# Two of eight contraction pairs of w_up by seven block products, in blocks of 1024 features

## The chip, the cores and the metric

The kernel runs on one core of one Trainium2 chip. The time is the device time of that core in microseconds (us). Three runs of the kernel before gave 1325.3, 1325.52 and 1325.8 us; the median is 1325.52 us.

## The reference

One layer of a hybrid decoder block on x of 256 tokens by 2048 features, all in float32. It computes an RMSNorm, a wide input projection, two token mixers (an mLSTM of 4 heads and a block-sparse attention of 8 heads), a gated merge, `x = x + merged @ w_out`, and then the MLP, which is the part at stake here:

```
hn = rms_norm(x, norm_mlp)                                # (256, 2048)
x  = x + square(relu(hn @ w_up)) @ w_down                 # w_up (2048, 8192), w_down (8192, 2048)
```

The two MLP products are 256x2048x8192 each; together they are the larger half of all the arithmetic.

## The kernel before

**Precision.** Every float32 operand of a product is split into a high part (what the matrix engine's reduced float32 format keeps) and a low part (the rest). A product is then three matmuls: high by high, high by low, low by high. The weights come from HBM into `raw` (4 slots of 1 MB), ScalarE copies the high part into `w_hi`, VectorE subtracts it from the raw value into `w_lo`. Both are rings of `RING = 4` slots, and one slot holds 128 x 1024 numbers.

**Steps.** The work of TensorE (PE) is a row of steps with one running number g. For each step ScalarE (ACT) makes w_hi (L477, L716), VectorE (DVE) makes w_lo (L785, L1117), and PE uses both. ACT waits for `w_used`, so that it writes step g only when PE has finished step g-4. DVE waits for `hi_made` of step g, and PE for `lo_made` of step g. All three engines run their own program strictly in order. Everything else that ACT and DVE must do (norms, reading PSUM, squares, transposes, splitting features) is a job that is written out by hand at a given step, ahead of that step's copy or subtraction: the functions `jobs`, `up_jobs`, `first_sums`, `add_shared`, `add_own`.

**The MLP.** It is done in two halves f = 0, 1 of 4096 features each. In a half, w_up comes first, in 8 blocks of 512 features (j). A block has 8 steps; a step is two contraction tiles of 128 by 512 columns and takes 12 matmuls (two row tiles of tokens, two contraction tiles, three products, `half_rows`, L1244 to L1246). The results of a block stand in two PSUM banks, and blocks alternate between banks 4, 5 and 6, 7. Then ACT takes the relu with the norm's scale from PSUM (L730), squares it in 16 pieces of 32 partitions, which also moves blocks between partitions (L740), DVE transposes within 32 x 32 blocks into banks 0 to 3 (L1148), ACT copies the high part (L746) and DVE subtracts for the low part (L1153).

**Seven products.** w_down is done in two passes (n = 0, 1) of 1024 output columns over all eight banks. The contraction is in 16 pairs of tiles. Ten pairs are whole: 2 steps of 12 matmuls. Six pairs (`SEVEN`) use seven block products in place of eight, after Strassen and Winograd: the 2 x 2 blocks are (two token tiles) x (two contraction tiles) for the features and (two contraction tiles) x (two column halves) for the weights. Such a pair has 4 steps of 6, 3, 6 and 6 matmuls, 21 in place of 24. Its price is on DVE: three sums of the weights (`first_sums`, L1136 and L1138, and L1121), 3.5 in place of 2 subtractions of 1024 columns, sums of features (L1157 to L1161 and L1166, L1167), and the adding up of shared banks (`add_shared`). Four of the banks (`OWN`) hold results of their own, the four of `SHARED` hold terms that several results share.

## Time and profile before

| | |
|---|---|
| median of three runs | 1325.52 us |
| the profiled execution | 1325.57 us |
| its span, first to last instruction | 1323.8 us |
| PE busy | 1319.8 us (100% of the span), 5962 matmuls |
| DVE busy | 1003.3 us (76%) |
| ACT busy | 792.2 us (60%) |
| granted TensorE clock | 1.00 throughout |
| DMA | 259.57 MB, 196 GB/s mean |

How to read it: matmuls are pipelined, so each lasts some 0.39 us while one starts every 0.23 us; an engine that is 100% busy by the count need not be at its peak. "Idle before" is the time that an engine sat idle ahead of an instruction, and the arrow names what ended it. A time of a group's row is the mean of one instruction; in a timeline the first number is the start, the second the duration of the row, and xN says how many instructions were merged into it.

### The profile page before, as it was taken

The page shows a single profiled execution, that of the slowest core. Times are in us where ns is not written, and L with a number is a line of the kernel's source. Part 1 is how long each engine was busy: PE and PEld are TensorE (multiplying, and loading weights), DVE is VectorE, ACT ScalarE, POOL GpSimd, SP SyncE. Part 2 cuts the span into 40 slices and gives each one's busy share as a digit, 9 for nine tenths or more (in the row PEclk, how much of TensorE's full clock was granted, in tenths as well). Part 3 has the DMA queues.
Part 4 walks back from the last instruction along what each step waited for, and adds up shares of the span by engine and source line. Part 5 has one row for each costly group of instructions (what it writes and reads, how often), then busy time and mean ns, then how long its engine had stood idle before and what let it go on. Part 6 is the DMA issues. An engine that isn't in the chain of part 4 may idle for free.

```text
span 1323.8 us, 15784 instructions
## 1 busy us (share of the span) xinstructions
PE 1319.8 (100%) x5962; PEld 1096.2 (83%) x5962; DVE 1003.3 (76%) x1314; ACT 792.2 (60%) x1129; POOL 16.5 (1%) x31
## 2 busy tenths in 40 slices
PE   9999999999999999999999999999999999999999
PEld 8988888888888888888888888888888888888887
DVE  6788699777477874999856565999865565689986
ACT  6656554566545444354587878555536878775553
POOL 0101000000000000000000000000000000000000
PEclk9999999999999999999999999999999999999999
DMA  9656555555556665564665665565666666546563
GB/s 318 203 181 212 193 192 183 191 174 176 179 170 197 242 212 194 173 212 170 219 195 191 191 192 189 183 212 184 218 222 191 191 193 192 196 165 208 196 216 129
DMA packets 115173, 259.57 MB, mean 196 GB/s; under 512 B 4334, under 2 KB 7452, under 8 KB 114844
## 3 DMA queue, kind: packets, MB, share of 16 engines
q1 hardware_dynamic: 115068, 258.57, 59.4%
q8 instruction: 47, 0.77, 0.2%
q14 instruction: 26, 0.21, 0.0%
q10 hardware_dynamic: 32, 0.01, 0.0%
HBM read 256.46 MB, written 2.10 MB: 195 GB/s over the span
## 4 chain that ended last, share of the span: by engine, by line
PE 100%; DVE 0%; issue 0%
PE ps L1244 23%; PE ps L1246 23%; PE ps L1245 23%; PE ps L1254 8%; PE ps L1255 8%; PE ps L1256 8%; PE ps L1399 1%; PE ps L1380 1%; PE ps L1348 1%; PE ps L1344 1%; PE ps L1346 1%; PE ps L1354 0%; PE ps L1419 0%; PE ps L1470 0%; PE ps L1436 0%; PE ps L1418 0%
## 5 line engine op out<-in xcount | busy, mean ns | idle before, releaser
L785 DVE TENSOR_TENSOR w_lo<-raw,w_hi 128x1024 fp32r<-128x1024 f32 (+1 forms) x349 | 424.5, 1224 | 246.3 <-ACT w_hi L477 241.7
L477 ACT ACTIVATE w_hi<-raw 128x1024 fp32r<-128x1024 f32 (+1 forms) x349 | 368.2, 1062 | 319.9 <-PE ps L1246 302.5
L1244 PE MATMUL ps<-w_hi,xT 128*128 128x512 f32 x1088 | 425.7, 391 | 0.0
L1246 PE MATMUL ps<-w_hi,xT 128*128 128x512 f32 x1088 | 423.5, 389 | 0.0
L1245 PE MATMUL ps<-w_lo,xT 128*128 128x512 f32 x1088 | 423.3, 389 | 0.0
L1246 PEld LDWEIGHTS ps<-w_hi,xT 128*128 128x128 f32 x1088 | 204.2, 188 | 42.8
L1244 PEld LDWEIGHTS ps<-w_hi,xT 128*128 128x128 f32 x1088 | 204.3, 188 | 41.9
L1245 PEld LDWEIGHTS ps<-w_lo,xT 128*128 128x128 f32 x1088 | 204.3, 188 | 41.8
L716 ACT ACTIVATE w_hi<-raw 128x1024 fp32r<-128x1024 f32 (+1 forms) x152 | 147.9, 991 | 85.9 <-PE ps L1256 69.8
L1117 DVE TENSOR_TENSOR w_lo<-raw,w_hi 128x1024 fp32r<-128x1024 f32 (+1 forms) x152 | 168.0, 1138 | 41.3 <-ACT w_hi L716 39.4
L740 ACT ACTIVATE gate<-gate 32x256 f32<-32x256 f32 x256 | 106.0, 414 | 3.4
L1256 PE MATMUL ps<-w_hi,merged 128*128 128x512 f32 (+1 forms) x210 | 81.5, 388 | 0.0
L1255 PE MATMUL ps<-w_lo,merged 128*128 128x512 f32 (+1 forms) x210 | 81.5, 388 | 0.0
L1254 PE MATMUL ps<-w_hi,merged 128*128 128x512 f32 (+1 forms) x210 | 81.3, 387 | 0.0
L1255 PE MATMUL ps<-w_lo,branch 128*128 128x512 f32 x208 | 81.1, 390 | 0.0
L1256 PE MATMUL ps<-w_hi,branch 128*128 128x512 f32 x208 | 81.1, 390 | 0.0
L1254 PE MATMUL ps<-w_hi,branch 128*128 128x512 f32 x208 | 81.0, 389 | 0.0
L803 DVE STREAM_TRANSPOSE ps<-attn 32x256 f32<-32x256 f32 (+1 forms) x176 | 71.7, 407 | 2.9
L716 ACT ACTIVATE w_hi<-gate 128x1024 fp32r<-128x1024 f32 x24 | 25.5, 1062 | 45.0 <-PE ps L1256 45.0
L1244 PE MATMUL ps<-w_hi,branch 128*128 128x512 f32 x128 | 49.8, 389 | 0.0
L1245 PE MATMUL ps<-w_lo,branch 128*128 128x512 f32 x128 | 49.8, 389 | 0.0
L1246 PE MATMUL ps<-w_hi,branch 128*128 128x512 f32 x128 | 49.8, 389 | 0.0
(243 smaller groups left out, 1396.2 us busy)
## 6 DMA issues: line engine op xcount, KB each, us to landing
raw<-in_w_in_dram SPq DMA_DIRECT2D x73, 1024.0 KB, 5.1
raw<-in_w_up_dram SPq DMA_DIRECT2D x64, 1024.0 KB, 5.3
raw<-in_w_down_dram SPq DMA_DIRECT2D x64, 1024.0 KB, 5.1
raw<-in_w_out_dram SPq DMA_DIRECT2D x16, 1024.0 KB, 5.1
raw<-in_w_branch_b_dram SPq DMA_DIRECT2D x8, 1024.0 KB, 5.3
raw<-in_w_branch_a_dram SPq DMA_DIRECT2D x8, 1024.0 KB, 5.3
raw<-in_w_in_dram SPq DMA_DIRECT2D x4, 1040.0 KB, 9.0
rows<-in_x_dram SPq DMA_DIRECT2D x1, 2048.0 KB, 10.0
```

What stands on the lines that cost most here:

```text
L477: act.activation(dst[:, k % RING, :, :], src[:, k // 2, KH * (k % 2):KH * (k % 2) + KH, :], ACT.Copy).then_inc(hi_made, 1)
L716: act.activation(dst[:, 0:src.shape[-1]], src, ACT.Copy).then_inc(hi_made, 1)
L740: last = act.activation(moved[32 * q:32 * q + 32, r // 32, :, :, :], read[r:r + 32, q, :, :, :], ACT.Square)
L785: dve.tensor_tensor(lo[:, k % RING, :, :], src[:, k // 2, KH * (k % 2):KH * (k % 2) + KH, :], hi[:, k % RING, :, :].bitcast(F32), ALU.subt ...
L803: turned = dve.transpose(dst[q:q + 32, :, :, r:r + 32], src[r:r + 32, :, :, q:q + 32])
L1117: dve.tensor_tensor(lo, src, hi.bitcast(F32), ALU.subtract).then_inc(lo_made, 1)
L1244: pe.matmul(o, hi, w_hi[:, s, i, :], start=first, stop=False)
L1245: pe.matmul(o, hi, w_lo[:, s, i, :], start=False, stop=False)
L1246: last = pe.matmul(o, lo, w_hi[:, s, i, :], start=False, stop=end)
L1254: pe.matmul(ps[:, bank, out], a_hi, w_hi[:, s, c, cols], start=start, stop=False)
L1255: pe.matmul(ps[:, bank, out], a_hi, w_lo[:, s, c, cols], start=False, stop=False)
L1256: return pe.matmul(ps[:, bank, out], a_lo, w_hi[:, s, c, cols], start=False, stop=end)
```

## The change

A half f now has six blocks q. Blocks 0 to 3 are w_up in 1024 features each (before: eight of 512), and blocks 4 and 5 are the two passes of w_down. A w_up block goes over all eight banks, like a pass of w_down: eight pairs of contraction tiles, of which pairs 3 and 5 (`X_SEVEN`) go by seven products in 4 steps, and the other six are whole, in 2 steps each. So a w_up block has 20 steps (s0 to s19 in what follows). In block 0 the order of pairs is 0, 1, 2, 4, 3, 5, 6, 7, so steps s8 to s15 are the two seven-product pairs; in blocks 1 to 3 it is 0 to 7 and they are s6 to s9 and s12 to s15. Block 5 has its pairs in a new order with the same pattern of whole and seven.

What comes with it:

- `x_jobs`: the sums of the features hn of pairs 3 and 5, once for each half (x = 0, 1), at steps s5 and s6 of the first block 0 and at s18 and s20 of block 5 of the first half. DVE adds high and low part (128x512), makes four sums of 128 columns, ACT copies the high parts (128x512), DVE subtracts the low parts (128x512).
- the jobs on the results of block b: at its step s19 ACT copies a shared bank (`up_first`) and DVE makes four additions of 512 columns; at s3 of the next block DVE adds the own banks (2 of 128x1024); at s4 ACT takes the relu (2 of 128x1024, from SBUF); from s5 on ACT squares in 16 pieces of 32x512, two in a step of a whole pair and one in a step of a seven-product pair, so until s16 (in block 4 until s15); in the two steps after the last square DVE transposes (128x1024 each, within SBUF; before into PSUM); ACT's high parts one step after each; DVE's low part and the sums for w_down 3 and 5 steps after the last square, and the low parts of those sums 5 and 7 steps after it.
- ACT and DVE run one loop over all steps of the MLP; SP's loads of w_up are written out (they were a loop) and bring two tiles of 1024 columns in place of four tiles of 512, again 1 MB each.

```diff
 SEVEN = (3, 5, 7, 9, 11, 13)
-ORDER = ((0, 1, 2, 4, 6, 3, 5, 8, 7, 10, 9, 11, 12, 13, 14, 15), (0, 3, 1, 5, 2, 7, 4, 9, 6, 11, 8, 13, 10, 12, 14, 15))
-PARTS = [[4 if i in SEVEN else 2 for i in ORDER[n]] for n in range(2)]
-DOWN = sum(PARTS[0]) + sum(PARTS[1])
-FB = 8 + DOWN // 8
-OWN, SHARED = (4, 0), (0, 4)
+X_SEVEN = (3, 5)
+UP = 4
+ORDER = ((0, 1, 2, 4, 3, 5, 6, 7), (0, 1, 2, 3, 4, 5, 6, 7), (0, 1, 2, 3, 4, 5, 6, 7), (0, 1, 2, 3, 4, 5, 6, 7),
+         (0, 1, 2, 4, 6, 3, 5, 8, 7, 10, 9, 11, 12, 13, 14, 15), (0, 13, 14, 3, 15, 5, 1, 7, 2, 9, 4, 11, 6, 8, 10, 12))
+PARTS = [[4 if i in (X_SEVEN if q < UP else SEVEN) else 2 for i in ORDER[q]] for q in range(6)]
+STEPS = [sum(p) for p in PARTS]
+HALF = sum(STEPS)
+LOADS = (0, 2, 4, 6, 8, 12)
+OWN, SHARED = (4, 0, 4, 0, 4, 0), (0, 4, 0, 4, 0, 4)
...
-        up_pos = gate_f[:, 0:1024]
-        up_sq = gate_f[:, 1024:2048]
-        w_diff = gate_f[:, 0:1024]
+        merged_f = attn.rearrange("p (t a c) -> p t a c", a=2, c=S)
+        x_pair, x_sums = (attn[:, 512 * t:512 * t + 512] for t in (14, 15))
+        x_ops = merged[:, 10:14, :, :].rearrange("p t a c -> p (t a c)").rearrange("p (x o a c) -> p x o a c", x=2, a=2, c=P)
...
+        def step_of(f, q, at, part=0):
+
+            return 8 * B_UP + HALF * f + sum(STEPS[:q]) + sum(PARTS[q][:at]) + part
...
+        def square_steps(f, b):
+
+            g, left, steps = end_of(f, b) + 6, 16, []
+            while left:
+                seven = PARTS[place_of(g)[1]][place_of(g)[2]] == 4
+                steps.append((g, min(left, 1 if seven else 2)))
+                left -= steps[-1][1]
+                g += 1
+            return steps
+
+        def squared(f, b):
+
+            return square_steps(f, b)[-1][0]
+
+        def x_sums_step(f, x):
+
+            return 8 * B_UP + 5 + x if f == 0 else step_of(0, 5, ORDER[5].index(15), 1) + 5 + 2 * x
...
+            def up_jobs(f, b, g):
+
+                end, sq_end = end_of(f, b), squared(f, b)
+                feat, tiles = (branch_f, merged_f)[b // 2], slice(8 * (b % 2), 8 * (b % 2) + 8)
+                if g == step_of(f, b, last_shared(b), 3) + 4:
+                    act.wait_ge(w_used, step_of(f, b, last_shared(b), 1) + 1)
+                    if b >= 1:
+                        act.wait_ge(up_kept, 4 * f + b)
+                    elif f == 1:
+                        act.wait_ge(shared_read, 2)
+                    act.activation(part_sums[:, 0, :], ps[:, SHARED[b], :], ACT.Copy).then_inc(up_first, 1)
+                if g == end + 5:
+                    if (f, b) == (0, 0):
                         act.wait_ge(x2_scaled, 1)
-                        if f == 1:
-                            act.wait_ge(shared_read, 2)
                     for m in range(M):
-                        last = act.activation(up_pos[:, N * m:N * m + N], ps[:, 4 + 2 * u + m, :], ACT.Relu,
-                                              scale=x2_r[:, m:m + 1])
-                    last.then_inc(up_read, 1)
...
+                        act.wait_ge(up_read, 8 * f + 2 * b + m + 1)
+                        last = act.activation(feat[:, tiles, 1, P * m:P * m + P],
+                                              gate_f[:, 1024 * m:1024 * m + 1024].rearrange("p (t c) -> p t c", c=P),
+                                              ACT.Relu, scale=x2_r[:, m:m + 1])
+                    last.then_inc(up_kept, 1)
+                done = 0
+                for at, count in square_steps(f, b):
+                    for o in range(done, done + count):
+                        if g != at:
+                            continue
+                        if o == 0:
+                            act.wait_ge(up_kept, 4 * f + b + 1)
+                        r, q = o // 4, o % 4
+                        read = feat[:, tiles, 1, :].rearrange("p t (m q c) -> p q m t c", m=M, q=4)
+                        moved = feat[:, tiles, 0, :].rearrange("p t (m q c) -> p q m t c", m=M, q=4)
+                        last = act.activation(moved[32 * q:32 * q + 32, r, :, :, :], read[32 * r:32 * r + 32, q, :, :, :],
...
+                        if o == 15:
+                            last.then_inc(up_squared, 1)
+                    done += count
+                for c in range(2):
+                    j = 2 * b + c
+                    if g == sq_end + 2 + c:
+                        act.wait_ge(up_turned, 8 * f + j + 1)
+                        act.activation((branch, merged)[j // 4][:, 4 * (j % 4):4 * (j % 4) + 4, 0, :], feat_f(j)[:, :, 1, :],
+                                       ACT.Copy).then_inc(up_hi, 1)
+                    if g == sq_end + 5 + 2 * c and 2 * j + 1 in SEVEN:
+                        p, t = SEVEN.index(2 * j + 1), 4 * j + 2
+                        act.wait_ge(up_lo_made, 8 * f + j + 1)
+                        act.wait_ge(pair_sum, len(SEVEN) * f + p + 1)
+                        act.activation((branch, merged)[t // 16][:, t % 16, 0, P:S], sums[:, 0, :], ACT.Copy)
+                        act.activation(sum_ops(2 * j + 1)[:, :, 0, :], sums[:, 1:4, :], ACT.Copy).then_inc(pair_hi, 1)
...
+            def pair_sums(out, a11, a21, a12, a22):
+
+                dve.tensor_tensor(out[2], a11, a21, ALU.subtract)
+                link(dve.tensor_tensor(out[0], a21, a22, ALU.add))
+                link(dve.tensor_tensor(out[1], out[0], a11, ALU.subtract))
+                return dve.tensor_tensor(out[3], a12, out[1], ALU.subtract)
+
+            def x_jobs(f, x, g):
+
+                if g == x_sums_step(f, x):
+                    i = X_SEVEN[x]
+                    if f == 0:
+                        dve.wait_ge(w_used, 8 * B_UP)
+                        dve.wait_ge(x2_lo, i // 2 + 1)
+                    else:
+                        dve.wait_ge(w_used, step_of(0, 5, ORDER[5].index(15), 1) + 1)
+                    if x:
+                        dve.wait_ge(x_ops_lo, 2 * f + x)
+                    pair = xT[:, 2 * i:2 * i + 2, :, :].bitcast(F32)
+                    v = x_pair.rearrange("p (t c) -> p t c", c=S)
+                    link(dve.tensor_tensor(v, pair[:, :, 0, :], pair[:, :, 1, :], ALU.add))
+                    pair_sums([x_sums[:, P * o:P * o + P] for o in range(4)],
+                              *(v[:, t, P * m:P * m + P] for t in range(2) for m in range(M))).then_inc(x_summed2, 1)
+                    dve.wait_ge(x_ops_hi, 2 * f + x + 1)
+                    dve.tensor_tensor(x_ops[:, x, :, 1, :], x_sums.rearrange("p (o c) -> p o c", c=P),
+                                      x_ops[:, x, :, 0, :].bitcast(F32), ALU.subtract).then_inc(x_ops_lo, 1)
+
+            def up_jobs(f, b, g):
+
+                sq_end = squared(f, b)
+                if g == step_of(f, b, last_shared(b), 3) + 4:
+                    sh = SHARED[b]
+                    dve.wait_ge(up_first, 4 * f + b + 1)
+                    dve.wait_ge(w_used, step_of(f, b, last_shared(b), 3) + 1)
+                    link(dve.tensor_tensor(part_sums[:, 3, :], part_sums[:, 0, :], ps[:, sh + 2, :], ALU.add))
+                    dve.tensor_tensor(part_sums[:, 1, :], part_sums[:, 3, :], ps[:, sh + 1, :], ALU.add)
+                    link(dve.tensor_tensor(part_sums[:, 2, :], part_sums[:, 3, :], ps[:, sh + 3, :], ALU.add))
+                    dve.tensor_tensor(part_sums[:, 3, :], part_sums[:, 2, :], ps[:, sh + 1, :],
+                                      ALU.add).then_inc(up_shared, 1)
+                if g == end_of(f, b) + 4:
+                    dve.wait_ge(up_shared, 4 * f + b + 1)
+                    dve.wait_ge(w_used, end_of(f, b) + 1)
+                    for m in range(M):
+                        own = OWN[b] + 2 * m
+                        c = gate_f[:, 1024 * m:1024 * m + 1024]
+                        dve.tensor_tensor(c, c, banks(own, own + 2), ALU.add).then_inc(up_read, 1)
+                for c in range(2):
+                    j = 2 * b + c
+                    ft = feat_f(j)
+                    hi_lo = (branch, merged)[j // 4][:, 4 * (j % 4):4 * (j % 4) + 4, :, :]
+                    if g == sq_end + 1 + c:
+                        dve.wait_ge(up_squared, 4 * f + b + 1)
+                        dve.transpose(*(ft[:, :, a, :].rearrange("p t (b c) -> p t b c", c=32) for a in (1, 0)))\
+                           .then_inc(up_turned, 1)
+                    if g == sq_end + 3 + 2 * c:
+                        if 2 * j + 1 in SEVEN:
+                            dve.wait_ge(up_turned, 8 * f + j + 1)
+                            p = len(SEVEN) * f + SEVEN.index(2 * j + 1)
+                            if p:
+                                dve.wait_ge(pair_lo, p)
+                            pair_sums([sums[:, o, :] for o in range(4)],
+                                      *(ft[:, t, 1, P * m:P * m + P] for t in (2, 3) for m in range(M))).then_inc(pair_sum, 1)
+                            dve.wait_ge(pair_sum, p + 1)
+                        dve.wait_ge(up_hi, 8 * f + j + 1)
+                        dve.tensor_tensor(hi_lo[:, :, 1, :], ft[:, :, 1, :], hi_lo[:, :, 0, :].bitcast(F32),
+                                          ALU.subtract).then_inc(up_lo_made, 1)
+                    if g == sq_end + 5 + 2 * c and 2 * j + 1 in SEVEN:
+                        p = SEVEN.index(2 * j + 1)
+                        dve.wait_ge(pair_hi, len(SEVEN) * f + p + 1)
+                        a, ops = hi_lo[:, 2, :, P:S], sum_ops(2 * j + 1)
+                        dve.tensor_tensor(a[:, 1, :], sums[:, 0, :], a[:, 0, :].bitcast(F32), ALU.subtract)
+                        dve.tensor_tensor(ops[:, :, 1, :], sums[:, 1:4, :], ops[:, :, 0, :].bitcast(F32),
+                                          ALU.subtract).then_inc(pair_lo, 1)
...
+                for q in range(6):
+                    if q == 0 and f == 1:
...
+                    elif 0 < q <= UP:
+                        pe.wait_ge(up_shared, 4 * f + q)
+                    elif q > UP:
...
+                    for at, i in enumerate(ORDER[q]):
+                        if (f, q) == (0, 0):
+                            pe.wait_ge(x2_lo, max(3, i // 2 + 1))
+                        if q == 0 and i in X_SEVEN:
+                            pe.wait_ge(x_ops_lo, 2 * f + X_SEVEN.index(i) + 1)
+                        if q == UP:
...
+                        if PARTS[q][at] == 4:
+                            seven_pair(f, q, at)
```

## Rows read from the trace of the kernel before

**Rows 1.** Page, parts 1 and 2: busy time of engines, and granted clock by slices.
```profile
PE 1319.8 (100%) x5962; PEld 1096.2 (83%) x5962; DVE 1003.3 (76%) x1314; ACT 792.2 (60%) x1129; POOL 16.5 (1%) x31
...
PEclk9999999999999999999999999999999999999999
```

**Rows 2.** Page, part 4 (chain that ended last), and all waits of PE.
```profile
PE 100%; DVE 0%; issue 0%
...
PE ps L1470 <- DVE ahead L1045: 1.0, 1, 1.0
```

**Rows 3.** Timeline of ACT: w_hi in two successive steps of w_up.
```profile
654.20 1.06 ACT L477 ACTIVATE w_hi<-raw 128x1024 fp32r<-128x1024 f32 x1 [0.73 <-PE ps L1246]
656.92 1.06 ACT L477 ACTIVATE w_hi<-raw 128x1024 fp32r<-128x1024 f32 x1 [1.66 <-PE ps L1246]
```

**Rows 4.** Timeline of DVE: w_down, one seven-product pair behind another.
```profile
864.72 1.23 DVE L1136 TENSOR_TENSOR gate<-raw 128x1024 f32<-128x1024 f32 x1
865.98 0.69 DVE L1138 TENSOR_TENSOR raw<-raw,gate 128x512 f32<-128x512 f32 x1
866.71 2.96 DVE L1117 TENSOR_TENSOR w_lo<-raw,w_hi 128x1024 fp32r<-128x1024 f32 x3
869.59 0.68 DVE L1121 TENSOR_TENSOR raw<-raw 128x512 f32<-128x512 f32 x1
870.19 1.22 DVE L1117 TENSOR_TENSOR w_lo<-gate,w_hi 128x1024 fp32r<-128x1024 f32 x1
871.40 1.23 DVE L1117 TENSOR_TENSOR w_lo<-raw,w_hi 128x1024 fp32r<-128x1024 f32 x1
```

**Rows 5.** Timeline of PE at the same place.
```profile
867.58 0.40 PE L1256 MATMUL ps<-w_hi,sums_b 128*128 128x512 f32 x1
867.99 0.50 PE L1254 MATMUL ps<-w_hi,sums_b 128*128 128x512 f32 x1
```

**Rows 6.** Groups by line and shape, DVE, 650 to 1323 us (busy us, mean ns).
```profile
L1148 DVE STREAM_TRANSPOSE ps<-gate 128x1024 f32<-128x1024 f32 x16 | 20.0, 1253 | 0.0
L1153 DVE TENSOR_TENSOR branch<-ps,branch 128x1024 fp32r<-128x1024 f32 x8 | 9.7, 1218 | 0.0
L1194 DVE TENSOR_TENSOR rows<-rows,ps 128x1024 f32<-128x1024 f32 x6 | 7.0, 1215 | 0.3 <-PE ps L1256 0.3
L1179 DVE TENSOR_TENSOR gate<-gate,ps 128x512 f32<-128x512 f32 x4 | 2.7, 682 | 0.0
L1161 DVE TENSOR_TENSOR sums<-ps,sums 128x128 f32<-128x128 f32 x12 | 3.5, 291 | 0.4
L1167 DVE TENSOR_TENSOR sums_b<-sums,sums_b 128x384 fp32r<-128x384 f32 x8 | 4.4, 552 | 0.0
```

**Rows 7.** The same for ACT, 632 to 1323 us.
```profile
L716 ACT ACTIVATE w_hi<-raw 128x1024 fp32r<-128x1024 f32 x128 | 133.1, 1059 | 76.3 <-PE ps L1256 60.2 <-DVE raw L1121 7.4 <-PE ps L1246 7.3
L740 ACT ACTIVATE gate<-gate 32x256 f32<-32x256 f32 x256 | 106.0, 414 | 3.4
L716 ACT ACTIVATE w_hi<-raw 128x512 fp32r<-128x512 f32 x24 | 15.1, 631 | 9.7 <-PE ps L1256 9.7
```

**Rows 8.** Timeline of DVE in the first steps of w_up.
```profile
645.28 3.75 DVE L803 STREAM_TRANSPOSE ps<-rows 32x256 f32<-32x256 f32 x8
649.06 1.22 DVE L785 TENSOR_TENSOR w_lo<-raw,w_hi 128x1024 fp32r<-128x1024 f32 x1
650.66 1.66 DVE L791 SCALAR_TENSOR_TENSOR xT<-ps,g_col,xT 128x256 fp32r<-128x256 f32 x4 [0.38 <-ACT xT L695]
652.24 2.35 DVE L785 TENSOR_TENSOR w_lo<-raw,w_hi 128x1024 fp32r<-128x1024 f32 x2
```

**Rows 9.** Groups by line and shape, DVE, 0 to 640 us.
```profile
L803 DVE STREAM_TRANSPOSE ps<-attn 32x256 f32<-32x256 f32 x112 | 51.0, 456 | 1.8
...
L813 DVE STREAM_TRANSPOSE ahead<-prob 32x192 f32<-32x192 f32 x64 | 23.6, 369 | 1.0
L803 DVE STREAM_TRANSPOSE ps<-attn 32x128 f32<-32x128 f32 x64 | 20.6, 323 | 1.1
```

338 lines of the change are left out of this document (139 added, 199 removed).

## The prediction, made before the changed kernel ran

> **What bounds the kernel now.** I read the page first: PE is busy for 100% of the span and its clock is granted in full in every slice [rows 1]. Pipelined matmuls make "busy" a weak word, so the chain of waits and PE's own waits come next. The chain is PE alone, and the only wait of PE in the whole execution is 1.0 us at its start [rows 2]. Then the cadence: in w_up two copies to w_hi, each released by PE, start 2.72 us apart [rows 3], so a step of 12 matmuls costs 2.72 us and a matmul 0.2267 us. The kernel is bound by the number of matmuls, and each taken away is worth 0.2267 us as long as PE goes on without a wait. So the second question is how near the other engines are to becoming late. In w_down, where seven-product pairs stand already, they nearly are: DVE needs from 864.72 to 871.40, 6.68 us, for one such pair [rows 4], and PE only 21 x 0.2267 = 4.76 us. Where two such pairs follow each other PE waits already: the matmul at 867.99 starts 0.41 us after the one before it, 0.06 us after the end of the first w_lo of the group that starts at 866.71 (866.71 + 1.22 = 867.93) [rows 4, 5].
>
> **What is removed.** Two pairs in each of eight w_up blocks lose 3 matmuls each: 8 x 2 x 3 = 48, times 0.2267 = 10.9 us, all of it on PE's path.
>
> **What is added, per w_up block.** DVE costs are distances between starts of successive instructions, since they overlap by some 0.07 us: w_lo 1.15, of 512 columns 0.58, weight sums 1.26 and 0.73 and 0.60, w_lo of the difference 1.21 [rows 4]. A block of 20 steps takes DVE 12 x 1.15 + 2 x 6.68 = 27.2 us. To this come the jobs. Two additions of own banks are 2.4 (1215 ns each) and four of shared banks 2.65 (682 ns each, two linked to the one ahead). Two transposes at 1.16 (1253 ns less the overlap) and two low parts of features at 1.15 (1218) follow. For six of eight groups of 512 features there are sums for w_down: four additions at 291 ns with their links 1.15, low parts 0.7 [rows 6]. That is 27.2 + 2.4 + 2.65 + 2.3 + 2.3 + up to 3.7 = 35.7 us while block 1 runs, 39.9 in block 2, 40.6 in block 3. PE needs 186 x 0.2267 = 42.2. It fits on average with 2 to 6 us to spare. But the lead is small, and DVE cannot use all its time.
>
> **The lead.** ACT may copy step g only when PE has finished g-4, and the copy (1.06) and the subtraction (1.22) take 2.31 with the semaphores. w_lo must be there 0.25 us before PE's finish of g-1. The steps g-3 to g-1 last 8.16 us among whole pairs, so the lead is at most 5.6 us. They last 1.36 + 0.68 + 1.36 or the like, 3.40, for the last step of a seven-product pair and the first two after its third step, so there the lead is at most 0.85 us, however fast DVE was before. I go through a block with these numbers, time 0 being PE's finish of the block before (PE finishes s5 at 16.32, s6 at 17.68, s9 at 21.08, s10 at 23.80, s15 at 31.28, s19 at 42.16).
> - Steps s9 to s11, blocks 1 to 3. ACT copies s9 at 16.32 to 17.38. Two squares of 32x512 follow. The trace has 32x256 at 414 ns, and copies that grow by 0.84 ns per column from 512 to 1024 [rows 7]; my estimate from these is 0.63 us each (bounds: 0.41 as for 256 columns, 1.06 as for a full copy). The copy of s10 then runs from 18.55 to 19.61 in place of 17.68 to 18.74, its w_lo ends at 20.86 where 20.83 is the limit, the two weight sums (1.99) and w_lo for s11 end at 24.0 where 23.55 is the limit: PE waits 0.55 with 0.1 for its restart.
> - Steps s16 to s19. DVE is free at 31.54 and must have w_lo of s19 by 39.74 + 0.55 of the wait above included, so in 8.2 us. It has two transposes, three w_lo, a feature low part and the shared additions: 2 x 1.16 + 3 x 1.15 + 1.15 + 2.65 = 9.6 us in block 1, and 10.8 in blocks 2 and 3, where sums for w_down come to it. PE waits 1.6, 2.8 and 2.8 us.
> - The surplus is worked off in s0 to s5 of the next block: DVE must catch up 2.8 us and has 8.8 us of other jobs there against 16.3 us of PE. It is in time by 0.15 us at s1, so no wait there, and from s9 on the pattern is the same again.
> So block 1 costs 2.1 us of waits, blocks 2 and 3 cost 3.4 each.
> - Block 4 (first pass of w_down) takes over block 3's results in its two successive seven-product pairs, s10 to s17. From 32.24 on (after s15) DVE has 14.5 us of work until w_lo of s20, and PE wants it at 41.9: two transposes 2.3, two w_lo and one of the difference 3.5, sums and low parts 4.25, weight sums 2.0, two more w_lo 2.4. The waits at s16 to s22 and s29 add to 5.8; 0.3 of it is there now [rows 5], so 5.5 net.
> Both halves have this: 2 x (2.1 + 3.4 + 3.4 + 5.5) = 28.8 us.
>
> **The sums of hn (x_jobs).** In the first half they stand at s5 and s6, behind the jobs of w_out's last block. There DVE ends its eight transposes at 649.03, w_lo of s5 at 650.28, and w_lo of s6 at 652.24 + 1.22 = 653.46 [rows 8], which is 0.5 us ahead of the limit (PE finishes s5 at 654.20, when the copy of s9 starts [rows 3]). In between comes, for each x: an addition of 512 (0.73), four of 128 (1.13), then DVE waits for ACT's 128x512 (0.63, [rows 7]), and ACT, which waits for DVE's sums first, makes the copy of that step only after it (1.06). So w_lo of s5 ends at 653.8 and of s6 at 660.4, 6.9 us later than now. PE waits 2.7 and 3.9 us. With no lead left, the seven-product pairs at s8 to s15 cost 0.4 and 0.9 more, together 7.9. For the second half they stand at s18 and s20 of block 5, right behind and right at seven-product pairs: 2.6 + 0.4 + 2.0 + 0.3 = 5.2 us. In block 0 of the second half DVE has only two additions besides, and nothing waits. Sum 13.1 us. Bounds for all this: nothing if the lead hid it, and 2 x 2 x 3.5 = 14 if none of it did.
>
> **Other edits.** Loads of 1 MB stay, with four slots and at least three pairs of time, over 13 us, ahead of each; SP's written-out waits have nothing behind them but the next load. ACT's load in a block (12 x 1.06 + 2 x 3.8 for copies, 16 x 0.63, and 6 us of other jobs) is some 36 us of 42.2, and counts only where said above. The new order of block 5 has the same pattern. The tail is the same. All nothing.
>
> **Sum.** 28.8 + 13.1 = 41.9 us of waits, less 10.9: +31.0. The profiled execution (1325.57) becomes 1356.6, and the median, 0.05 less, 1356.5.
>
> **A rule on transposes.** The rows have no difference between SBUF and PSUM as target: 32x192 within SBUF takes 369 ns, between 323 for 128 and 456 for 256 columns into PSUM [rows 9]. The Trainium skill, VectorE: DVE Perf Modes, "The perf-mode tier table", says that float32 operations with one source go at twice the rate if both ends are in SBUF; it lists copies, not transposes. By it the 16 moved transposes would be 0.5 us shorter each, and the sum some 8 us less, 1348.
>
> **Rivals.**
> A, the lead hides it. If DVE's jobs at the ends of blocks cost 8 us or less between s16 and s19, and the two sums of hn stay within the lead, PE's waits fall under 10.9 us and the kernel gets faster: at none, 1314.6. For it: DVE's total of 36 to 41 us is below PE's 42.2, and w_down at nearly the same density waits 0.3 us now. Against it: the 0.5 us of lead at s6, and 8.2 us against 9.6 or 10.8 at the end of a block. Point of decision: waits of 10.9 us in all.
> B, half of it. The waits of the sums and of block 4 come, those at block ends mostly do not (if the overlap of DVE instructions is larger there): 13.1 + 11 = 24 less 10.9, 1338.7.
> C, the change saves nothing because PE's real cadence in seven-product pairs is slower: the gaps in w_down are 0.2267 too, so this goes into the forecast's range.
> D, PE's clock. The longest wait of PE now is 1.0 us and the clock stays at 1.00, the level of 2.4 GHz [rows 1, 2]; the new ones last up to 3.9. If each of the nine waits of over 2 us were followed by one step at the lower level, 1.2 GHz, where 12 matmuls take 2.72 more, the time is up to 24 us longer: 1381; some of it gives DVE its lead back, so 1370. The Trainium skill, TensorE: Matmul & The Clock Gate, Part 1, says that the gate falls to half rate when PE has idled; no row here shows it.
>
> **Chances.** Forecast 0.63 (own range 1346 to 1366, from the bounds of the squares and the transposes), B 0.16, D 0.06, A 0.11, and 0.04 for waits that just cancel the saving. A difference below 0.2% (2.65 us) cannot be told from none. Faster 0.11, same 0.04, slower 0.85. The range 1333 to 1368 leaves out A, most of D and little else.
>
> **What would show it.** 48 matmuls fewer; PE's waits for DVE w_lo summing to some 40 us, the longest in the first block 0 at s5 and s6, then at s19 of blocks 1 to 3 and s16 to s20 of block 4; none in the first half of a block and none in block 0 of the second half; clock 1.00; DVE nearly without idle time from s10 of one block to s3 of the next. Wrong would be PE waits under 11 us, transposes of 0.7 us, squares far from 0.63, or a clock below 1.

## The result, and the profile after

The changed kernel takes 1364.74 us (median of four runs, 1363.01 to 1367.62), the kernel before 1325.57 us on the same chip: a ratio of 1.030 with a 95% interval of [1.028, 1.032]. It is slower by 39.2 us, where 31.0 were forecast. The profiled run is the slowest of the four, 1367.62 us with a span of 1364.7.

First the page of the changed kernel (busy time, clock by slices, chain), to be laid beside [rows 1, 2], and all waits of PE (us in total, times, longest):

```profile
PE 1331.4 (98%) x5914; PEld 1092.0 (80%) x5914; DVE 1112.0 (81%) x1454; ACT 796.6 (58%) x1029; POOL 16.5 (1%) x31
...
PEclk9999999999999999999899999999999999999999
...
PE 82%; DVE 9%; ACT 7%; issue 2%; ACTq 0%; DVEq 0%
```
```profile
PE ps L1362 <- DVE w_lo L1180: 28.2, 23, 3.6
PE ps L1571 <- DVE ahead L1104: 1.0, 1, 1.0
```

5962 - 5914 = 48 matmuls are gone, as counted. The chain is no longer PE alone: 16% of it is DVE and ACT, and PE has 23 waits for a w_lo that were not there. DVE's busy time grew by 109 us and is still only 81%, so no total explains the result; the place of the waits must.

The list of waits counts 28.2 us, and that is not all: it leaves out the time between the end of a wait and PE's normal pace, and waits under some tenths. So I also read all starts of matmuls from 640 us on. Of the distance to the matmul before I take what exceeds 0.2267 us by more than 0.01, and call it clock where the distance is 0.41 to 0.435 (behind the second wait below, at granted clock 0.50, matmuls start 0.427 apart) and wait elsewhere. The kernel before has 0.6 us by this count, the changed one 41.1 us of waits and 9.6 us (48 matmuls) of clock. 41.1 + 9.6 - 0.6 - 10.9 = 39.2. That this is the difference of the medians to the tenth is chance: the count is of the profiled run, whose span is 40.9 us longer than before. The other 1.7 us are 0.5 ahead of 640 us and distances too small for the count. The rule for clock is rough as well: 47 of the 48 matmuls lie in stretches where the trace has a granted clock of 0.50, and where it is 1.00 such a distance is a short wait. By block (us, f is the half):

| block | forecast | waits | clock |
|---|---|---|---|
| f0, 0 | 7.9 | 6.8 | 2.2 |
| f0, 1 / 2 / 3 | 2.1 / 3.4 / 3.4 | 2.5 / 3.8 / 4.0 | 0 / 1.0 / 1.2 |
| f0, 4 / 5 | 5.5 / 5.2 | 4.8 / 3.5 | 2.0 / 1.6 |
| f1, 0 | 0 | 0 | 0 |
| f1, 1 / 2 / 3 | 2.1 / 3.4 / 3.4 | 2.6 / 3.7 / 4.0 | 0 / 0 / 1.4 |
| f1, 4 | 5.5 | 5.4 | 0.2 |
| sum | 41.9 | 41.1 | 9.6 |

Next the sums of hn at s5 and s6 of the first block, DVE's timeline and then ACT's and PE's (start, duration):

```profile
649.60 0.69 DVE L1225 TENSOR_TENSOR attn<-xT 128x512 f32<-128x512 f32 x1
...
651.18 0.29 DVE L1210 TENSOR_TENSOR attn<-attn 128x128 f32<-128x128 f32 x1
652.17 0.69 DVE L1229 TENSOR_TENSOR merged<-attn,merged 128x512 fp32r<-128x512 f32 x1 [0.70 <-ACT merged L816]
653.12 1.22 DVE L1180 TENSOR_TENSOR w_lo<-raw,w_hi 128x1024 fp32r<-128x1024 f32 x1 [0.25 <-ACT w_hi L760]
...
659.65 1.23 DVE L1180 TENSOR_TENSOR w_lo<-raw,w_hi 128x1024 fp32r<-128x1024 f32 x1 [0.26 <-ACT w_hi L760]
```
```profile
651.51 0.63 ACT L816 ACTIVATE merged<-attn 128x512 fp32r<-128x512 f32 x1 [8.08 <-DVE attn L1210]
652.04 1.04 ACT L760 ACTIVATE w_hi<-raw 128x1024 fp32r<-128x1024 f32 x1
```
```profile
651.54 0.39 PE L1364 MATMUL ps<-w_hi,xT 128*128 128x512 f32 x1
654.39 0.50 PE L1362 MATMUL ps<-w_hi,xT 128*128 128x512 f32 x1 [2.47 <-DVE w_lo L1180]
...
657.04 0.39 PE L1364 MATMUL ps<-w_hi,xT 128*128 128x512 f32 x1
661.02 0.76 PE L1362 MATMUL ps<-w_hi,xT 128*128 128x512 f32 x1 [3.59 <-DVE w_lo L1180]
661.58 0.63 PE L1363 MATMUL ps<-w_lo,xT 128*128 128x512 f32 x1
662.01 0.63 PE L1364 MATMUL ps<-w_hi,xT 128*128 128x512 f32 x1
662.43 0.63 PE L1362 MATMUL ps<-w_hi,xT 128*128 128x512 f32 x1
```

One can follow the hand-over from engine to engine: DVE's last sum ends at 651.47, ACT's copy of it runs 651.51 to 652.14, DVE's low part waits for that (0.70), ACT's w_hi for this very step comes only behind it (652.04 to 653.08), DVE waits again (0.25), and w_lo of s5 ends at 654.34; PE starts 0.05 later. [Rows 8] had w_lo end at 650.28. At s6 it is 660.88 against 653.46. Behind the second wait matmuls start 0.43 us apart and last 0.63 in place of 0.39: the lower clock.

And the end of block 2 (s19), DVE and PE:

```profile
766.74 1.24 DVE L1257 STREAM_TRANSPOSE branch_f<-branch_f 128x1024 f32<-128x1024 f32 x1
767.90 1.18 DVE L1180 TENSOR_TENSOR w_lo<-raw,w_hi 128x1024 fp32r<-128x1024 f32 x1
769.00 1.24 DVE L1257 STREAM_TRANSPOSE branch_f<-branch_f 128x1024 f32<-128x1024 f32 x1
...
772.43 1.23 DVE L1269 TENSOR_TENSOR branch<-branch_f,branch 128x1024 fp32r<-128x1024 f32 x1
773.57 0.68 DVE L1239 TENSOR_TENSOR gate<-gate,ps 128x512 f32<-128x512 f32 x1
...
775.61 0.69 DVE L1242 TENSOR_TENSOR gate<-gate,ps 128x512 f32<-128x512 f32 x1
776.21 2.35 DVE L1180 TENSOR_TENSOR w_lo<-raw,w_hi 128x1024 fp32r<-128x1024 f32 x2
```
```profile
774.96 0.39 PE L1364 MATMUL ps<-w_hi,xT 128*128 128x512 f32 x1
777.49 0.50 PE L1362 MATMUL ps<-w_hi,xT 128*128 128x512 f32 x1 [2.14 <-DVE w_lo L1180]
```

From 766.74 on DVE has no gap, and PE waits from 775.2. All the work there is short and known; it stands in four steps. Before that, from s10 to s16, DVE is not pressed: there it waits four times for ACT's w_hi, 0.4 to 1.2 us each.

### The profile page after: what moved, and what is told of

It is laid out like the page before. It is cut to its first block, busy times and chain, and to the rows that moved or that the text cites. A ratio compares the mean times of both kernels' runs of the same rounds, so it can differ in the third digit from the quotient of the medians.

```text
span 1364.7 us, 15521 instructions
## 1 busy us (share of the span) xinstructions
PE 1331.4 (98%) x5914; PEld 1092.0 (80%) x5914; DVE 1112.0 (81%) x1454; ACT 796.6 (58%) x1029; POOL 16.5 (1%) x31
## 4 chain that ended last, share of the span: by engine, by line
PE 82%; DVE 9%; ACT 7%; issue 2%; ACTq 0%; DVEq 0%
PE ps L1354 14%; PE ps L1352 14%; PE ps L1353 14%; PE ps L1362 12%; PE ps L1363 12%; PE ps L1364 12%; ACT w_hi L760 4%; DVE w_lo L1180 4%; ACT branch_f L792 1%; PE ps L1500 1%; ACT attn L792 1%; PE ps L1481 1%; DVE branch_f L1257 1%; DVE attn L1257 1%; PE ps L1449 1%
## 5 line engine op out<-in xcount | busy, mean ns | idle before, releaser
L1180 DVE TENSOR_TENSOR w_lo<-raw,w_hi 128x1024 fp32r<-128x1024 f32 (+1 forms) x296 | 331.5, 1148 | 79.4 <-ACT w_hi L760 76.7
L517 ACT ACTIVATE w_hi<-raw 128x1024 fp32r<-128x1024 f32 (+1 forms) x221 | 232.7, 1062 | 241.4 <-PE ps L1354 232.2
L844 DVE TENSOR_TENSOR w_lo<-raw,w_hi 128x1024 fp32r<-128x1024 f32 (+1 forms) x221 | 268.1, 1223 | 119.5 <-ACT w_hi L517 117.2
L760 ACT ACTIVATE w_hi<-raw 128x1024 fp32r<-128x1024 f32 (+1 forms) x296 | 290.3, 998 | 122.8 <-PE ps L1364 105.1
L1352 PE MATMUL ps<-w_hi,xT 128*128 128x512 f32 x576 | 226.6, 393 | 0.0
L1354 PE MATMUL ps<-w_hi,xT 128*128 128x512 f32 x576 | 224.3, 389 | 0.0
L1353 PE MATMUL ps<-w_lo,xT 128*128 128x512 f32 x576 | 224.2, 389 | 0.0
L1362 PE MATMUL ps<-w_hi,xT 128*128 128x512 f32 x432 | 174.1, 403 | 19.6 <-DVE w_lo L1180 18.4
L1363 PE MATMUL ps<-w_lo,xT 128*128 128x512 f32 x432 | 171.1, 396 | 0.0
L1364 PE MATMUL ps<-w_hi,xT 128*128 128x512 f32 x432 | 170.8, 395 | 0.0
L1354 PEld LDWEIGHTS ps<-w_hi,xT 128*128 128x128 f32 x576 | 108.1, 188 | 22.8
L1353 PEld LDWEIGHTS ps<-w_lo,xT 128*128 128x128 f32 x576 | 108.2, 188 | 22.0
L1352 PEld LDWEIGHTS ps<-w_hi,xT 128*128 128x128 f32 x576 | 108.2, 188 | 21.7
L1362 PEld LDWEIGHTS ps<-w_hi,xT 128*128 128x128 f32 x432 | 82.4, 191 | 47.3 <-DVE w_lo L1180 26.5
L1362 PE MATMUL ps<-w_hi,merged 128*128 128x512 f32 (+1 forms) x274 | 107.1, 391 | 3.8 <-DVE w_lo L1180 3.8
L1364 PE MATMUL ps<-w_hi,merged 128*128 128x512 f32 (+1 forms) x274 | 107.1, 391 | 0.0
L1363 PE MATMUL ps<-w_lo,merged 128*128 128x512 f32 (+1 forms) x274 | 107.1, 391 | 0.0
L1364 PEld LDWEIGHTS ps<-w_hi,xT 128*128 128x128 f32 x432 | 82.8, 192 | 17.9
L1363 PEld LDWEIGHTS ps<-w_lo,xT 128*128 128x128 f32 x432 | 82.8, 192 | 16.7
L1362 PE MATMUL ps<-w_hi,branch 128*128 128x512 f32 x208 | 82.5, 397 | 4.6 <-DVE w_lo L1180 4.5
L1363 PE MATMUL ps<-w_lo,branch 128*128 128x512 f32 x208 | 82.1, 395 | 0.0
L1364 PE MATMUL ps<-w_hi,branch 128*128 128x512 f32 x208 | 81.9, 394 | 0.0
```

Of the source, the lines that this page charges most:

```text
L517: act.activation(dst[:, k % RING, :, :], src[:, k // 2, KH * (k % 2):KH * (k % 2) + KH, :], ACT.Copy).then_inc(hi_made, 1)
L760: act.activation(dst[:, 0:src.shape[-1]], src, ACT.Copy).then_inc(hi_made, 1)
L844: dve.tensor_tensor(lo[:, k % RING, :, :], src[:, k // 2, KH * (k % 2):KH * (k % 2) + KH, :], hi[:, k % RING, :, :].bitcast(F32), ALU.subt ...
L1180: dve.tensor_tensor(lo, src, hi.bitcast(F32), ALU.subtract).then_inc(lo_made, 1)
L1352: pe.matmul(o, hi, w_hi[:, s, i, :], start=first, stop=False)
L1353: pe.matmul(o, hi, w_lo[:, s, i, :], start=False, stop=False)
```

## The experiments

Each kernel is the changed one with the edit shown (the main lines of it; `...` marks what is left out). The table gives all of them but 10, which ran once. Waits and clock are counted as above from the profiled run, the time is the median of four. "Fewer matmuls" is the saving by them in us.

| kernel | time (us) | ratio to before [95%] | fewer matmuls | waits + clock |
|---|---|---|---|---|
| changed | 1364.74 | 1.030 [1.028, 1.032] | 10.9 | 41.1 + 9.6 |
| 1 no sums of hn | 1353.19 | 1.021 [1.019, 1.023] | 10.9 | 32.9 + 4.0 |
| 2 w_up without seven products | 1337.39 | 1.009 [1.007, 1.011] | 0 | 8.9 + 3.4 |
| 3 squares respaced | 1359.02 | 1.025 [1.024, 1.027] | 10.9 | 37.9 + 6.0 |
| 4 sums of hn on GpSimd | 1357.17 | 1.025 [1.023, 1.026] | 10.9 | 35.6 + 5.0 |
| 5 features' sums on GpSimd | 1368.02 | 1.032 [1.030, 1.033] | 10.9 | 43.2 + 10.4 |
| 6 edits of 3, 4, 5 together | 1342.2 | 1.012 [1.010, 1.014] | 10.9 | 25.5 + 3.2 |
| 7 edits of 2 and 5 | 1342.29 | 1.013 [1.011, 1.014] | 0 | 15.5 + 0.4 |
| 8 as 2, jobs spread in block 4 | 1331.55 | 1.005 [1.003, 1.006] | 0 | 5.7 + 0.8 |
| 9 one seven pair in w_up, jobs bunched | 1350.05 | 1.018 [1.016, 1.019] | 5.4 | 24.9 + 4.6 |
| 11 one seven pair, jobs spread | 1336.78 | 1.009 [1.007, 1.010] | 4.1 | 14.4 + 0.6 |

In each row 1325.6, less the saving, plus waits and clock, is the time within 2 us. So these terms carry all that differs but for 2 us. In 7, 8 and 11 the trace has a granted clock of 1.00 throughout the MLP: their 0.4, 0.8 and 0.6 us of "clock" are short waits.

**1. The sums of hn left out.**

```diff
-                    for x in range(2):
-                        x_jobs(f, x, g)
```

> The changed kernel without x_jobs: the sums of hn of pairs 3 and 5, their high parts on ACT and low parts on DVE are left out in both halves, so the seven-product pairs of w_up multiply whatever stands in x_ops. Theory (lead: a job of DVE costs PE time only where the work behind it does not fit into the lead that the ring of four leaves): the waits of the first block 0 (6.9 us, and 2.2 us of matmuls at the lower clock behind them) and of block 5 of the first half (3.5 and 1.6 us) go but for some 0.3 us, nothing else changes: 14 us less, 1351. Rival 1 (DVE is simply overloaded, and each microsecond of DVE work counts wherever it is): the four sums take DVE about 2.9 us each, so 11 to 12 us less, and waits at the ends of w_up blocks get shorter as well. Rival 2 (the seven products or the blocks over eight banks cost PE time by themselves): at most 2 us less.

It fell by 11.6 us, which as a time is what rival 1 said and 2.4 short of the theory; the places decide between them. Block 0 of the first half goes from 6.8 to 1.0 us of waits and block 5 from 3.5 to nothing; the waits at the ends of the other blocks do not get shorter, as rival 1 wanted, but stay the same to 0.3 us. So the waits are local to a block (block 4 of the first half gains 0.6). Within block 0 they are not: the 1.0 us is nearly all a wait at s11 (0.9) that the changed kernel does not have: there DVE is idle for 1.0 us at 667.6, behind the waits at s5 and s6, and here it has no such pause. Between the two profiled runs the span falls by 13.9 us, 8.2 of it waits and 5.6 clock; the medians lie closer, since the changed kernel's profiled run is its slowest.

**2. w_up without seven products.** All eight pairs whole; own banks are copied and not added.

```diff
-X_SEVEN = (3, 5)
+X_SEVEN = ()
```

> The changed kernel with no pair of w_up by seven products (X_SEVEN empty): w_up stays in blocks of 1024 features over four own banks, all eight pairs whole, no sums of hn, no shared banks to add up, DVE copies the own banks to SBUF in place of adding them. w_down as in the changed kernel. Theory (lead): 48 matmuls come back (10.9 us), DVE has 10 us less to do in each block of w_up, all waits of w_up and block 5 go, block 4 keeps at most 3 us: 1326 to 1330. Rival 2 (the wide blocks, squares of 512 columns within SBUF, transposes in SBUF or the written-out loads cost time by themselves): above 1335.

A miss. PE's waits in w_up are gone, but block 4 keeps 4.5 and 4.3 us of waits:

```profile
PE ps L1356 <- DVE w_lo L1175: 6.8, 6, 1.9
```

So some 12 of the 39 us do not come from seven products in w_up, as rival 2 had it. They come from the wider blocks, though only at one place: the last one leaves 1024 features to be turned and split (before, 512), and that falls on block 4's two successive seven-product pairs.

**3. Squares respaced.** Three in s5 and s6, none beside the limited steps s10 to s12; the transposes stay where they were.

```diff
-                steps.append((g, min(left, 1 if seven else 2)))
...
+            at = {5: 3, 6: 3, 7: 2, 8: 2, 9: 1, 13: 1, 14: 2, 15: 2} if b < 3 else {s: 2 for s in range(5, 13)}
```

> Only the steps change at which ACT squares the results of a block: 3, 3, 2, 2, 1 in s5 to s9, none in s10 to s12, 1, 2, 2 in s13 to s15 for blocks 1 to 3; 2 in each of s5 to s12 of block 4. The transposes and all that follows stay at their steps, no work is added or taken away on any engine. Theory (lead): the copies of s10, s11 and s16 are no longer late by two squares (1.26 us), the waits at s10, s11 and s16 go, and DVE reaches s17 some 1.4 us earlier, so the wait at s19 falls from 0.9 to about 0.3 us in block 1 and from 2.1 to about 1.4 in blocks 2 and 3: about 2 us less in each of six blocks, 1352 to 1354. Rival 1 (DVE overloaded by its amount of work): DVE's work is the same, so no change, 1363 to 1366.

It fell by 5.7 us, between the two. DVE's work is the same, so rival 1 is out. Block 1 goes from 2.5 to 0.6 us. In blocks 2 and 3 the waits at s10 (0.35) and s16 (0.6) go, the one at s11 falls from 0.4 to 0.15 and the one at s19 from 2.4 to 1.8, as the theory said; but their sums come to 3.4 and 4.3, hardly less than 3.8 and 4.0, since a new wait has come at s8, 1.1 us in block 2 and 2.0 in block 3. There ACT's copy is late: ACT has no pause from s5 to s9 and twice has three squares ahead of a copy, and DVE waits 1.07 us for the copy of s8. ACT, then PE, in block 2:

```profile
741.69 1.92 ACT L787 ACTIVATE branch_f<-branch_f 32x512 f32<-32x512 f32 x3
```
```profile
750.31 0.50 PE L1357 MATMUL ps<-w_hi,merged 128*128 128x512 f32 x1 [0.87 <-DVE w_lo L1175]
```

So the squares were made late for one place and too dense for another. The 1.8 us that are left at s19 are what the amount of DVE's work between s16 and s19 costs (forecast: 10.8 us of work in 8.2).

**4. The sums of hn on GpSimd.** The same additions and low parts, issued by `pool`; ACT's high parts stand at s22 and s32 in block 5.

```diff
-                    link(dve.tensor_tensor(v, pair[:, :, 0, :], pair[:, :, 1, :], ALU.add))
...
+                link(pool.tensor_tensor(v, pair[:, :, 0, :], pair[:, :, 1, :], ALU.add))
```

> The sums of hn and their low parts are made by GpSimd instead of DVE, in the first half before w_up begins, in the second half during block 5; ACT's high parts stand at s5, s6 and at s22, s32. Result as in the changed kernel. Theory (lead): DVE and ACT no longer wait for each other there, so the same 14 us go as with the sums left out: 1351. Rival 3 (GpSimd and DVE hinder each other at SBUF): DVE's subtraction of 1024 columns goes above 1.22 us while GpSimd works, and the gain is under 10 us.

The time is 1357.17 us, 7.6 better than the changed kernel, and worse by 4 than leaving them out, so the theory missed and rival 3 held. DVE's timeline while GpSimd works, and what GpSimd did:

```profile
939.94 1.48 DVE L1243 TENSOR_TENSOR gate<-raw 128x1024 f32<-128x1024 f32 x1
941.46 0.83 DVE L1245 TENSOR_TENSOR raw<-raw,gate 128x512 f32<-128x512 f32 x1
942.32 5.29 DVE L1222 TENSOR_TENSOR w_lo<-raw,w_hi 128x1024 fp32r<-128x1024 f32 x3
```
```profile
937.61 1.32 POOL L503 TENSOR_TENSOR attn<-attn 128x128 f32<-128x128 f32 x1
938.90 1.44 POOL L504 TENSOR_TENSOR attn<-attn 128x128 f32<-128x128 f32 x1
...
944.97 2.10 POOL L521 TENSOR_TENSOR attn<-xT 128x512 f32<-128x512 f32 x1
```

The same three operations of DVE took 1.23, 0.69 and 2.96 us in [rows 4]. DVE is slowed to 5.29 / 2.96 = 1.8 times while GpSimd reads. The Trainium skill, SBUF — State Buffer, "Who interferes with whom", says that a DVE instruction with two SBUF inputs and a GpSimd instruction that reads SBUF need the same port and that one blocks the other; the rows agree that they collide. That one blocks the other for the whole of an instruction they do not show: most of DVE's took 1.0 to 1.5 times as long, the longest 2.31 us for 1.22.

**5, 6 and 7. More on GpSimd.** In 5 the sums and low parts of features go there, in 6 the edits of 3 and 4 too, in 7 the edits of 2 and 5. In 6 and 7 the transposes of block 3's features also move, to s18 and s24 of block 4, and what follows them with it.

```diff
-                            pair_sums([sums[:, o, :] for o in range(4)],
...
+                pool_pair_sums([sums[:, o, :] for o in range(4)],
...
-                        dve.tensor_tensor(hi_lo[:, :, 1, :], ft[:, :, 1, :], hi_lo[:, :, 0, :].bitcast(F32),
...
+                pool.tensor_tensor(hi_lo[:, :, 1, :], ft[:, :, 1, :], hi_lo[:, :, 0, :].bitcast(F32),
```

> The sums of features for w_down, the low parts of features and of these sums are made by GpSimd instead of DVE (per w_up block two subtractions of 1024 columns, and for six of eight groups four additions of 128 and two subtractions); ACT's high parts of the sums stand 6 and 12 steps after the last square. Sums of hn stay on DVE. Result as in the changed kernel. Theory (lead): DVE has 2.3 us less between s16 and s19 and up to 3 us less in s1 to s3, so the wait at s19 goes in block 1 and falls from 2.1 to some 0.2 us in blocks 2 and 3, block 4 keeps about half of its 5 us: 15 us less, 1350. Rival 3 (GpSimd takes SBUF time from DVE: in the run with the sums of hn on GpSimd DVE's 1024 columns took 1.48 us beside it against 1.22): with some 20 us of GpSimd in each block DVE loses 4 us or more of the 6 that it saves, and the gain is under 8 us.

> All together: sums of hn and the features' sums and low parts on GpSimd, squares spaced as in the run before (none in s10 to s12), and in block 4 the transposes at s18 and s24 with what follows behind them. Result as in the changed kernel. Theory (lead) without any hindrance by GpSimd: all waits but 2 to 3 us go: 1317 to 1320, below the kernel before. With DVE slowed by a fifth for half of its time: about 12 to 15 us of waits are left, 1328 to 1332.

> No pair of w_up by seven products, as in the run with X_SEVEN empty (1337.4 us, all waits left in block 4), and the features' sums and low parts on GpSimd with the transposes in block 4 at s18 and s24. Theory: the 4.5 us of waits in each block 4, and the matmuls at the lower clock behind them, come only from the jobs of block 3's results that fall into two successive seven-product pairs of w_down; with these moved the time is that of the kernel before, 1325 to 1328. Rival: block 4 waits because w_down's order of pairs leaves DVE late whatever the jobs: 1334 or more.

The theory missed all three times; 5 and 7 fell where their rivals were, 6 above both of its ranges. 5 is no better than the changed kernel (blocks 2 and 3 of the first half wait 2.1 and 2.0 us in place of 3.8 and 4.0, but block 1 waits 4.4 in place of 2.5 and block 4 in the two halves 7.2 and 8.6 in place of 4.8 and 5.4), and 7 is slower than 2 by 4.9 us though DVE has less to do. The groups of block 4's w_lo, of kernel 7 and then of kernel 2 (busy, mean ns):

```profile
L1210 DVE TENSOR_TENSOR w_lo<-gate,w_hi 128x1024 fp32r<-128x1024 f32 x6 | 9.5, 1584 | 1.9 <-ACT w_hi L795 1.9
L1210 DVE TENSOR_TENSOR w_lo<-raw,w_hi 128x512 fp32r<-128x512 f32 x6 | 6.6, 1098 | 1.1 <-ACT w_hi L795 1.0
```
```profile
L1175 DVE TENSOR_TENSOR w_lo<-gate,w_hi 128x1024 fp32r<-128x1024 f32 x6 | 7.3, 1212 | 1.9 <-ACT w_hi L760 1.9
L1175 DVE TENSOR_TENSOR w_lo<-raw,w_hi 128x512 fp32r<-128x512 f32 x6 | 4.1, 686 | 1.1 <-ACT w_hi L760 1.0
```

The work taken from DVE comes back as slower subtractions (1584 for 1212 ns, 1098 for 686), at just the steps without lead. How much of the 4.9 us comes from the moved transposes was not tested. These three change DVE's speed and the places at once, so I drew nothing on the lead from them.

**8. Same work, other places.** Kernel 2 with the pairs of block 4 in natural order (whole and seven alternate) and block 3's jobs at s16, s22, s23, s28, s34, s40 of block 4, with the squares there spaced as blocks 1 to 3 have them in experiment 3.

```diff
-         (0, 1, 2, 4, 6, 3, 5, 8, 7, 10, 9, 11, 12, 13, 14, 15), (0, 13, 14,
+         (0, 1, 2, 3, 4, 5, 6, 7, 8, 9, 10, 11, 12, 13, 14, 15), (0, 13, 14,
...
-                    if g == sq_end + 1 + c:
+                    if g == (sq_end + 1 + c if b < 3 else end_of(f, b) + 1 + 16 + 6 * c):
```

> No pair of w_up by seven products (as in the run of 1337.4 us, where all waits stood in block 4), all jobs on DVE again, but in block 4 whole and seven-product pairs alternate (pairs in their natural order) and the jobs on block 3's results are spread over it: transposes at s16 and s22, sums for w_down at s23, low parts at s28 and s40, low parts of the sums at s34. Same work. Theory (lead: what counts is how much DVE work falls between two points at which the lead is small): at most one job of 1.2 us falls into each cycle of a whole and a seven-product pair, which leaves DVE idle for 1.1 us in the kernel before; waits of 1 to 3 us per half in place of 4.5, and no matmuls at the lower clock: 1328 to 1332. Rival (the work in block 4 is too much wherever it is): still 1336 to 1338.

```profile
PE ps L1354 <- DVE w_lo L1170: 2.2, 2, 1.1
```

As expected, 1331.55. The work is the same, and block 4's waits fell from 4.5 and 4.3 to 2.7 us in each half. The two stretches at granted clock 0.50 that kernel 2 has (some 3 us) are gone. Which of the three edits, order, jobs or squares, gave how much was not tested.

**9 and 11. One seven-product pair in each block of w_up**, with the jobs where kernel 8 has them (9), and spread one or two to a step from s14 to s4 (11; there pair 13 is whole in block 4).

```diff
-X_SEVEN = (3, 5)
+X_SEVEN = (5,)
```
```diff
+            at = {"turn": (14, 15), "hi": (15, 16), "sum": (16, 19), "lo": (16, 20), "pair_hi": (17, 21), "pair_lo": (18, 22)}
+            if b == 3:
+                at = {"turn": (16, 28), "hi": (17, 29), "sum": (22, -9), "lo": (34, 35), "pair_hi": (42, -9), "pair_lo": (43, -9)}
+            return end_of(f, b) + 1 + at[what][c]
```

> One pair in eight of w_up by seven products (pair 5, behind five whole pairs) in place of two, its sums of hn at s8 of the first block and at s41 of block 5, two squares in each of s5 to s12, block 4 as in the run before. 24 matmuls fewer than in the kernel before, 5.4 us. Result as in the changed kernel. Theory (lead): DVE has some 36 us of work in a block of 43.5 us, and the only seven-product pair stands where ten whole steps lie ahead of it, so w_up waits under 1 us in all; block 4 costs 2 to 6 us in both halves: 1322 to 1328. Rival 1 (each microsecond of DVE work counts): half the excess of the changed kernel over the one with no seven products, (1364.7 - 1337.4) / 2 = 14 above the run before, 1343.

> One seven-product pair (5) in each w_up block of 18 steps, squares two by two in s5 to s12, and the jobs behind it written out one or two to a step from s14 to s4 of the next block, so that no two of the long ones stand in one step; block 4 in the natural order (whole and seven-product pairs alternate), its jobs spread, and pair 13 whole there. 18 matmuls fewer than before: 4.1 us. Theory (the waits come from where the jobs stand, not from what they sum to): waits of PE in w_up under 3 us in all eight blocks together, in block 4 under 2 us a half, so 1322 to 1328, and it may be the first version with seven-product pairs in w_up that is not slower than the kernel before. Rival (a seven-product pair of w_up costs its block some 3.5 us of waits wherever the jobs stand, as in the run with one such pair and bunched jobs): 1340 to 1350.

All waits of PE for w_lo in 9 and in 11:

```profile
PE ps L1360 <- DVE w_lo L1175: 15.4, 12, 2.4
```
```profile
PE ps L1369 <- DVE w_lo L1185: 5.4, 6, 1.0
```

9 missed, with a time above its rival's 1343 too: two transposes, the sums of one group (of two in blocks 2 and 3), two low parts and the shared additions stood in s13 to s17, right behind the pair, and PE waits up to 2.5 us at s17. Spreading took this from 24.9 to 14.4 us of waits, and 13.3 us off the time; yet 1336.78 lies between my theory (1322 to 1328) and the rival (1340 to 1350). What is left is of three kinds. In blocks 2 and 3 of both halves the four shared additions in one step, s17, right behind sums and a low part in s16, still hold up the next w_lo. That is four times 1.15 us and the restart, 5.0 us; here DVE and PE in block 2:

```profile
764.14 0.69 DVE L1247 TENSOR_TENSOR gate<-gate,ps 128x512 f32<-128x512 f32 x1
764.74 1.22 DVE L1185 TENSOR_TENSOR w_lo<-raw,w_hi 128x1024 fp32r<-128x1024 f32 x1
```
```profile
764.64 0.39 PE L1371 MATMUL ps<-w_hi,xT 128*128 128x512 f32 x1
766.02 0.50 PE L1369 MATMUL ps<-w_hi,xT 128*128 128x512 f32 x1 [0.98 <-DVE w_lo L1185]
```

Twice 1.0 us stand at s8 of block 4, where ACT has no pause between the squares, as in experiment 3 (8 and 9 have the same squares in block 4 and no such wait; why was not looked into). The other 7.4 us are some 27 steps late by 0.2 to 0.3 us each, most of them beside seven-product pairs. In one of them, in block 4, DVE turns features at 844.19, w_lo of the step starts at 845.36 and ends at 846.58, and PE's first matmul of the step starts at 846.68, 0.14 us late, the next 0.09 later still. I had counted only steps with two long jobs; the forecast's 0.85 us of lead leaves no room for one.

**10. Matmuls to fill the two waits at s5 and s6**, run once, with a profile: 9 and 14 matmuls into a bank that is not in use.

```diff
+                    if (f, q) == (0, 0) and 2 * at + part in (5, 6):
+                        pe.wait_ge(kept[1], 16)
+                        for _ in range(9 if part else 14):
+                            pe.matmul(ps[:, 2, :], xT[:, 0, 0, 0:P], xT[:, 1, :, :].rearrange("p a c -> p (a c)"), start=True, stop=True)
```

> The changed kernel with PE kept busy where it waits longest: 9 matmuls of 512 columns (2.0 us) ahead of its wait for s5 and 14 (3.2 us) ahead of that for s6 of the first block 0, into a bank that nothing reads before it is started anew. If PE's idleness lowers the clock, the matmuls behind s6 (661 to 666 us) start 0.227 us apart, not 0.427, and granted clock is 1.00 there; the waits of DVE stay, so the step itself is no earlier. If something else lowers it (the level falls in that stretch whatever PE does), they stay 0.427 apart.

Stretches of PE in the changed kernel (window, length, busy of PE, PEld, DVE, ACT, GpSimd, then granted clock, DMA share, GB/s), and the same in this one:

```profile
656.00:662.00 6.00, 2.41 (x9) 1.66 (x8) 4.95 (x9) 3.96 (x5) 0.00 (x0) 0.79 0.41 159
662.00:666.00 4.00, 4.00 (x11) 3.12 (x10) 3.90 (x8) 0.03 (x1) 1.60 (x1) 0.50 0.22 48
777.50:778.90 1.40, 1.40 (x6) 1.16 (x7) 1.40 (x3) 0.00 (x0) 0.00 (x0) 1.00 0.39 53
779.00:782.30 3.30, 3.30 (x9) 2.61 (x8) 3.09 (x7) 0.52 (x2) 0.00 (x0) 0.50 0.79 294
```
```profile
656.00:662.00 6.00, 5.65 (x25) 4.34 (x25) 4.91 (x10) 4.00 (x5) 0.00 (x0) 1.00 0.41 157
662.00:666.00 4.00, 3.92 (x18) 2.88 (x17) 3.93 (x7) 1.06 (x1) 1.60 (x1) 1.00 0.23 47
```

DVE is as busy and w_lo as late in both, and only PE's idleness differs: 0.50, the level of 1.2 GHz, without filler, and 1.00, 2.4 GHz, with it. So at this place the lower clock is the price of PE's own idle time. The Trainium skill, TensorE: Matmul & The Clock Gate, Part 1, says that an idle array is gated to half rate; here the trace agrees. The time, 1364.63 in a single execution, cannot show a gain of 2.2 us.

The other rows are of the wait that ends at 777.49. There the clock is still 1.00 when PE starts again and falls 1.4 us later, to 0.50 from 778.9 to 782.3. The changed kernel has six such stretches: 659.5 to 666.3, which begins within the wait for s6, and one behind each of the waits that end at 777.49, 825.17, 870.69, 952.69 and 1184.39. Nine waits are over 2 us. Behind the one for s5 (2.6 us) the clock stays at 1.00 for 5 us, and behind 1138.33 and 1229.88 (2.3 and 2.0 us) it does not fall at all. In kernel 10 it stays at 1.00 behind the wait of block 4 that is the same as the one at 870.69 here. The four executions of the changed kernel had mean clocks of 0.991 to 0.995. So idle time of PE brings the lower clock at the one place tested, but whether a given wait is followed by slow matmuls differs from one execution to another.

## Why the prediction was right, and where it was off

The time came out within the forecast's own range (1346 to 1366), and for the most part by the mechanism that was forecast: waits at the places where the lead is short. Some of the nearness is luck. Blocks 1 to 3 wait 2.8 us more than forecast (20.6 for 17.8), block 4 0.8 less (10.2 for 11.0), the sums of hn 2.8 less (10.3 for 13.1), and these errors nearly cancel; and the clock, which the sum does not have, could have cost more.

- The saving: 48 matmuls, 10.9 us, and the sums of the table bear it out within 2 us.
- The squares: 630 ns for 32x512, as estimated between 0.41 and 1.06. The transposes within SBUF last 1237 ns, where [rows 6] have 1253 for the same size into PSUM:

```profile
L792 ACT ACTIVATE attn<-attn 32x512 f32<-32x512 f32 x64 | 40.3, 630 | 1.2
```
```profile
L1257 DVE STREAM_TRANSPOSE branch_f<-branch_f 128x1024 f32<-128x1024 f32 x8 | 9.9, 1237 | 0.0
```

  The rate that the Trainium skill, VectorE: DVE Perf Modes, "The perf-mode tier table", gives for copies does not carry over to these transposes: they are 16 ns shorter and not 0.5 us, and the 1348 falls away. The table's one-source operations at twice the rate are copies and tensor_scalar; it has a shuffle, with one source too, at the single rate.
- The lead: waits stand where the walk through the block put them. With the restart they are 0.35 and 0.38 us at s10 and s11 (forecast 0.55 in all), 0.6 at s16 (not forecast), at s19 1.2 us in block 1 and 2.4 to 2.6 in blocks 2 and 3 (forecast 1.6, 2.8, 2.8), none in block 0 of the second half. Rival A fails on both of its points, and B too: blocks 1 to 3 have 20.6 of the 41.1 us, 16.1 of them at s16 and s19. One sign of the forecast did not come: DVE is not "nearly without idle time from s10" but only from s17. Experiment 1 shows that a block's waits change those of other blocks by 0.6 us at most, and experiment 3 which limit acts at which step; 2 against 8 and 9 against 11 show that other places for nearly the same work are worth 6 and 13 us (with another order of pairs in 8, and one pair made whole in 11). They do not show that the amount is without weight: 11 still waits 14.4 us.
- The working gives DVE 35.7 us in block 1, though its terms without the sums for w_down add up to 36.9. It fits if one of the two low parts (1.15) is left to the next block, as its steps have it; and 2.6 + 0.4 + 2.0 + 0.3 is 5.3 and not 5.2. Nothing hangs on either.
- Block 4: 4.8 and 5.4 us for 5.5. Its longest wait in the first half stands right behind the low part of the features:

```profile
868.18 1.23 DVE L1269 TENSOR_TENSOR merged<-attn,merged 128x1024 fp32r<-128x1024 f32 x1
869.32 1.22 DVE L1180 TENSOR_TENSOR w_lo<-raw,w_hi 128x1024 fp32r<-128x1024 f32 x1
```
```profile
870.69 0.47 PE L1362 MATMUL ps<-w_hi,merged 128*128 128x512 f32 x1 [1.88 <-DVE w_lo L1180]
```

  The start before it is at 868.41, so the distance is 2.28 us, where [rows 5] have 0.41 for the longest.
- The sums of hn: 6.8 us in the first half for 7.9 (w_lo of s5 and s6 end at 654.34 and 660.88 where 653.8 and 660.4 were said). At s5 and s6 it is right to 0.2 us; what it added for s8 to s15, 0.4 and 0.9, was not there at all. In block 5 it is 3.5 for 5.2, the largest error among the waits. The first set costs 2.4 us at 952.69, near the 2.6 said; the second 0.6 in place of 2.0. I take it that in both places DVE gained lead in the wait just before. For block 0 experiment 1 bears this out (without the waits at s5 and s6 one of 0.9 us appears at s11), for block 5 no run tested it.
- The step that failed is the clock. The forecast has none of it, and rival D has it as another course of things, at 24 us or not at all. It is an addition to the same waits: 48 matmuls at the lower level cost 48 x 0.20 = 9.6 us. That is why the time is 8.2 us above the forecast while the waits are 0.8 under it. "A clock below 1" was among the forecast's signs of being wrong, and it came. D had the number of waits over 2 us right, nine, but not what follows them: six of the nine are followed by slow matmuls or have them close by, 7 or 8 each and once 11, 1.4 to 2.2 us, where D has 12 matmuls behind each. Which wait is followed by them stays open (experiment 10).

No version here beats the kernel before. The nearest with seven products in w_up, 11, loses 14.4 us to waits and saves 4.1. Whether the shared additions in two steps and one job fewer beside each pair would bring it under 1325.6 was not tried.

## What to carry to other kernels

In a ring that in-order engines fill for each other, the average load of the filling engine says little: go step by step, and compare each job with the lead that the ring leaves at that step; behind short steps this lead was 0.85 us here (worked out from the rows), and a job of 1.15 us there is a wait. Do so for every engine that fills the ring: squares moved away from one narrow place made a wait at another (experiment 3). A saving on the bounding engine that gives the next engine more work should be priced at that place first. Nearly the same work in other places gave 5.8 us (2 to 8) and 13.3 (9 to 11); work moved to an engine that slows the first one gave 7.6 in experiment 4, and lost 3.3 in 5. Where PE is going to wait for 2 us and more, the sum needs a range for matmuls at the lower clock behind it: here 1.4 to 2.2 us behind six of nine such waits.

## What the hardware showed that I had not expected

- GpSimd's float32 additions are slow and slow DVE down: 128x128 took 0.79 to 1.44 us there in the rows of experiment 4, against 0.29 on DVE, and three subtractions of DVE took 5.29 us beside it against 2.96.
- The clock's cost behind waits: 9.6 us behind 41.1 us of waits, 3.4 behind 8.9 (kernel 2), and none behind the 15.5 of kernel 7, whose longest is 2.2 us. It does not go with the sum of the waits.
- The clock can fall after PE has gone back to work: in the changed kernel at 778.9 us, 1.4 us behind the end of the wait.
